# X and the first weights alternately, narrow chunks with their weights loaded and tokens streamed, 32 bytes of padding ahead of the feed-forward operand

## The reference

```python
def dsa_mixer(h, w_in, q_g, k_g, w_out):       # layer a; b is attention without the index
    q, k, v, gate, qi, ki, wi = split_cols(h @ w_in, A_WIDTHS)   # 2048, 512, 512, 2048, 1024, 64, 16 columns
    ...
    score = einsum('bqh,bqhs->bqs', wib, relu(qi . ki))          # index scores, top-64 keys of each query
    _, sel = lax.top_k(score, n_keep)
    ...
    return (jax.nn.silu(gate) * o) @ w_out
```

## Time and profile before

| | us |
|---|---|
| median of 3 runs (2584.04 to 2587.59) | 2585.28 |
| profiled execution, own time | 2575.33 |
| its span in the profile | 2573.9 |
| TensorE busy | 2424.0 (94%) |
| TensorE weight loads | 1978.0 (77%) |
| VectorE busy | 1408.0 (55%) |
| ScalarE busy | 1160.6 (45%) |

### The profile page before, as it was taken

How to read it: one execution, slowest core, us unless ns; L and a number is a source line. 1 busy time by engine, 2 the same in 40 slices (tenths; PEclk the granted TensorE clock), 3 DMA queues, 4 the chain that set the end, 5 groups by cost and what they waited for, 6 DMA issues and landing times.

```text
span 2573.9 us, 27885 instructions
## 1 busy us (share of the span) xinstructions
PE 2424.0 (94%) x11424; PEld 1978.0 (77%) x11424; DVE 1408.0 (55%) x1955; ACT 1160.6 (45%) x1632; POOL 9.6 (0%) x17
## 2 busy tenths in 40 slices
PE   6999999999999987959989889999999999999998
PEld 5777788777788866847877778888888888888886
DVE  4475655655554467576556554565554545454454
ACT  4346644546644543333334444444544344433443
POOL 0000000000000000000000000000000000000000
PEclk9899999999999898989999999999999999999999
DMA  5444355544455442212254336555565555555653
GB/s 186 150 132 130 125 183 184 169 158 131 148 180 166 150 147 82 82 49 82 87 180 145 129 115 194 182 179 189 191 193 183 192 184 194 181 194 183 195 181 114
DMA packets 204223, 400.13 MB, mean 155 GB/s; under 512 B 12736, under 2 KB 12768, under 8 KB 203712
## 3 DMA queue, kind: packets, MB, share of 16 engines
q1 hardware_dynamic: 202016, 391.08, 46.5%
q0 software_dynamic: 1648, 6.32, 0.8%
q10 hardware_dynamic: 432, 0.95, 0.1%
HBM read 396.23 MB, written 2.10 MB: 155 GB/s over the span
## 4 chain that ended last, share of the span: by engine, by line
PE 86%; DVE 9%; ACT 4%; issue 1%; DMA 0%; SPq 0%; ACTq 0%; DVEq 0%
PE ACC L713 25%; PE ACC L715 25%; PE ACC L714 25%; PE TP L394 1%; DVE WL L1492 1%; DVE arena L1249 1%; DVE arena L1278 1%; ACT WH L1001 1%; PE PV L572 1%; PE SC L567 1%; PE PV L575 1%; PE SC L441 1%; PE PV L433 1%; PE SC L624 1%; PE TP L420 1%
## 5 line engine op out<-in xcount | busy, mean ns | idle before, releaser
L1492 DVE TENSOR_TENSOR WL<-W,WH 128x1024 fp32r<-128x1024 f32 (+1 forms) x752 | 901.6, 1202 | 666.0 <-ACT WH L1001 664.2
L1001 ACT ACTIVATE WH<-W 128x1024 fp32r<-128x1024 f32 (+1 forms) x752 | 781.3, 1041 | 822.2 <-PE ACC L715 822.2
L713 PE MATMUL ACC<-WH,XH 128*128 128x512 f32 (+2 forms) x2656 | 1084.6, 408 | 8.2 <-ACT arena L992 4.7
L715 PE MATMUL ACC<-WH,XL 128*128 128x512 f32 (+2 forms) x2656 | 1040.6, 392 | 0.0
L714 PE MATMUL ACC<-WL,XH 128*128 128x512 f32 (+2 forms) x2656 | 1039.6, 391 | 0.0
L713 PEld LDWEIGHTS ACC<-WH,XH 128*128 128x128 f32 x2656 | 509.8, 192 | 120.2 <-issue 13.4
L715 PEld LDWEIGHTS ACC<-WH,XL 128*128 128x128 f32 x2656 | 508.1, 191 | 107.2
L714 PEld LDWEIGHTS ACC<-WL,XH 128*128 128x128 f32 x2656 | 510.3, 192 | 92.8 <-issue 2.0
L713 PE MATMUL ACC<-WH,HH 128*128 128x512 f32 x352 | 139.8, 397 | 0.0
L715 PE MATMUL ACC<-WH,HL 128*128 128x512 f32 x352 | 139.0, 395 | 0.0
L714 PE MATMUL ACC<-WL,HH 128*128 128x512 f32 x352 | 139.0, 395 | 0.0
(11 more groups left out here) (281 smaller groups left out, 1586.4 us busy)
## 6 DMA issues: line engine op xcount, KB each, us to landing
W<-in_w_in SPq DMA_DIRECT2D x84, 1024.0 KB, 5.0
W<-in_a_w_in SPq DMA_DIRECT2D x48, 1024.0 KB, 5.1
W<-in_w_ffn_gate SPq DMA_DIRECT2D x44, 1024.0 KB, 5.2
W<-in_w_ffn_up SPq DMA_DIRECT2D x44, 1024.0 KB, 5.2
W<-in_w_ffn_down SPq DMA_DIRECT2D x44, 1024.0 KB, 5.1
W<-in_b_w_in SPq DMA_DIRECT2D x40, 1024.0 KB, 5.1
W<-in_a_w_out SPq DMA_DIRECT2D x16, 1024.0 KB, 5.0
W<-in_b_w_out SPq DMA_DIRECT2D x16, 1024.0 KB, 5.0
```

The source lines that it names most:

```text
L713: MM(out, hx, WH[:, k, 0:ch.width], start=q == 0 and k == 0, stop=False)
L715: ins = MM(out, lx, WH[:, k, 0:ch.width], start=False, stop=last and k == QK - 1)
L1001: A(M.WH[n % 2][:, ks, 0:ch.width], M.W[n % 4][:, ks, 0:ch.width], ACT.Copy).then_inc(*did("weights_rounded", n, half))
L1492: TT(M.WL[n % 2][:, ks, 0:ch.width], M.W[n % 4][:, ks, 0:ch.width], M.WH[n % 2][:, ks, 0:ch.width].bitcast(F32), ALU.subtract).then_inc(*d ...
```

## The change

Four things. X's column blocks and the first four quads are loaded in turn (X0, W0, X1, W1, ...); the identity is loaded by itself ahead, the rest of the constants later; two of X's blocks are turned ahead of the loop, interleaved with the rounding of quads 0 and 1, and the others, the squares, roots and tables become side work of the first chunk. The two narrow chunks become one quad each of 16 tiles, with the weights (80 or 40 columns) as stationary operand and the 256 tokens streamed; the result, with output columns on the partitions, is copied to M.NT, transposed by the new task `narrow` one visit behind the next chunk's first, and scaled into M.KW or M.NAR. c.nar now follows c.q0, `index` starts four visits behind a.kw and `dn_gates` three behind c.nar. And a tile of 32 bytes per partition is put between the small tiles and the arena.

```diff
-            add("a.kw", one(w, INDEX_COL + IH * ID, ID + IH), "act")
+            add("a.kw", one(w, INDEX_COL + IH * ID, ID + IH), "act", quads=1, tiles=D // P)
...
-    add("c.nar", [(w, GATE_COL, 3 * N2), (w, AB_COL, 2 * DH)], "act", fresh="x.c")
...
+            add(f"c.{n}{i}", one(w, DN_COL + c * DH * HD + i * CH), "act", fresh="x.c" if n + str(i) == "q0" else None)
+            if n + str(i) == "q0":
+                add("c.nar", [(w, GATE_COL, 3 * N2), (w, AB_COL, 2 * DH)], "act", quads=1, tiles=D // P)
...
+    for c in range(2, NC_D):
+        begin(4 * c - 6, "turn", "x.a", c)
+    for c in range(NC_D):
+        begin(8 + c, "squares", "a", c)
+    begin(11, "roots", "a")
+    begin(12, "tables", "a")
     begin(after("a.i0"), "index_rope", 0)
     begin(after("a.i1"), "index_rope", 1)
-    begin(after("a.kw"), "index")
+    begin(after("a.kw") + 1, "narrow", "a.kw")
+    begin(after("a.kw") + 4, "index")
...
-    begin(after("c.nar"), "dn_gates")
+    begin(after("c.nar") + 1, "narrow", "c.nar")
+    begin(after("c.nar") + 3, "dn_gates")
...
+def tiles_of(buffer, ch, half):
+
+    mine = buffer[:, half * HK:(half + 1) * HK, :]
+    if ch.tiles == QK:
+        return mine[:, :, 0:ch.width]
+    n = ch.tiles // 2
+    return mine.rearrange("p k n -> p (k n)")[:, 0:n * ch.width].rearrange("p (k n) -> p k n", k=n)
...
+    sb("to_64_bytes", [P, 8])
...
+    M.NT = {"a.kw": cut(6144, T), "c.nar": cut(12288, T)}
...
-    for c in range(NC_D):
-        sp.dma_start(M.X[:, :, c * CH:(c + 1) * CH], a["x"][0, :, c * CH:(c + 1) * CH].rearrange("(t p) d -> p t d", p=P)).then_inc(*did(f"x_landed{c}", by=16))
     for ch in K.chunks:
         for q in range(ch.quads):
             n = ch.first + q
+            if n < NC_D:
+                cs = slice(n * CH, (n + 1) * CH)
+                sp.dma_start(M.X[:, :, cs], a["x"][0, :, cs].rearrange("(t p) d -> p t d", p=P)).then_inc(*did(f"x_landed{n}", by=16))
...
-                src = a[w][0][row:row + QK * P, col:col + width].rearrange("(k p) n -> p k n", p=P)
+                src = a[w][0][row:row + ch.tiles * P, col:col + width].rearrange("(k p) n -> p k n", p=P)
+                if ch.tiles != QK:
+                    for half in range(2):
+                        ks = slice(half * ch.tiles // 2, (half + 1) * ch.tiles // 2)
+                        sp.dma_start(tiles_of(M.W[n % 4], ch, half)[:, :, place:place + width], src[:, ks, :]).then_inc(*did(f"weights_landed{n % 4}", n, place, half, by=16))
+                    place += width
+                    continue
...
-    pe.wait_ge(*at("consts_landed"))
-    for c in range(NC_D):
+    pe.wait_ge(*at("identity_landed"))
+    for c in range(2):
         for _ in turn("x.a", c):
             pass
...
+    def narrow(name):
+
+        w = K.width_of[name]
+        pe.wait_ge(*at("acc_taken_act", name, 0))
+        wait_empty("TP0")
+        for t in range(TB):
+            ins = TR(TP[0][:, t * w:(t + 1) * w], M.NT[name][0:w, t * P:(t + 1) * P], ident[0:w, 0:w])
+        ins.then_inc(*did("narrow_transposed", name))
+        emptied["TP0"] = ("narrow_taken", name)
+        yield
+
...
+        if ch.tiles != QK:
+            n, out = ch.first, M.ACC[0][0:ch.width, 0:T]
+            pe.wait_ge(*at(*taken[0], 0))
+            for part in range(4):
+                if part % 2 == 0:
+                    pe.wait_ge(*at("weights_rest", n, part // 2))
+                WH, WL = tiles_of(M.WH[n % 2], ch, part // 2), tiles_of(M.WL[n % 2], ch, part // 2)
+                for k in range(part * ch.tiles // 4, (part + 1) * ch.tiles // 4):
+                    j = k % (ch.tiles // 2)
+                    MM(out, WH[:, j, :], hi[:, k, :], start=k == 0, stop=False)
+                    MM(out, WH[:, j, :], lo[:, k, :], start=False, stop=False)
+                    ins = MM(out, WL[:, j, :], hi[:, k, :], start=False, stop=k == ch.tiles - 1)
+                ins.then_inc(*did("multiplied", n, part // 2, part % 2))
+                sides_of(tasks, K.starts, visit, live)
+                visit += 1
+            taken[0] = ("acc_taken_act", ch.name)
+            continue
...
-                    if q == 0 and half == 0 and taken:
-                        pe.wait_ge(*at(*taken, t))
+                    if q == 0 and half == 0 and taken[t]:
+                        pe.wait_ge(*at(*taken[t], t))
...
+        taken = [("acc_taken_" + ch.taker, ch.name)] * TB
...
+    def narrow(name):
+        w, to = K.width_of[name], {"a.kw": M.KW, "c.nar": M.NAR}[name]
+        act.wait_ge(*at("reciprocal_roots", name[0]))
+        act.wait_ge(*at("narrow_transposed", name))
+        for t in range(TB):
+            ins = A(to[:, t, :], TP[0][:, t * w:(t + 1) * w], ACT.Copy, scale=scale_of(name[0], t))
+        ins.then_inc(*did("narrow_taken", name))
+        yield
+
     def take(ch, t):
 
         l, name = ch.name[0], ch.name[2:]
+        if ch.tiles != QK:
+            if t == 1:
+                act.wait_ge(*at("multiplied", ch.first, 1, 1))
+                A(M.NT[ch.name][0:ch.width, :], M.ACC[0][0:ch.width, 0:T], ACT.Copy).then_inc(*did("acc_taken_act", ch.name, 0))
+            return
...
+            act.wait_ge(*at(f"weights_landed{n % 4}", n, ch.width - ch.parts[-1][2], *(() if ch.tiles == QK else (1,))))
...
+        A(tiles_of(M.WH[n % 2], ch, half), tiles_of(M.W[n % 4], ch, half), ACT.Copy).then_inc(*did("weights_rounded", n, half))
...
-    act.dma_start(M.consts[:, :], a["consts"]).then_inc(*did("consts_landed", by=16))
+    act.dma_start(M.ident, a["consts"][:, 0:P]).then_inc(*did("identity_landed", by=16))
...
-    act.dma_start(M.QKG.rearrange("p l n w -> p (l n w)"), a["qk_gains"].partition_broadcast(P)).then_inc(*did("qk_gains_landed", by=16))
     act.wait_ge(*at("gains_landed"))
     for n in range(2):
+        for _ in turn("x.a", n):
+            pass
         for half in range(2):
             round_up(n, half)
-    for c in range(NC_D):
-        for _ in turn("x.a", c):
-            pass
-    for c in range(NC_D):
-        for _ in squares("a", c):
-            pass
-    for _ in roots("a"):
-        pass
+    act.dma_start(M.consts[:, P:], a["consts"][:, P:]).then_inc(*did("consts_landed", by=16))
+    act.dma_start(M.QKG.rearrange("p l n w -> p (l n w)"), a["qk_gains"].partition_broadcast(P)).then_inc(*did("qk_gains_landed", by=16))
...
+        if l == "a":
+            dve.wait_ge(*at("consts_landed"))
+            dve.wait_ge(*at("qk_gains_landed"))
...
-        dve.wait_ge(*at("acc_taken_act", "a.kw", 1))
+        dve.wait_ge(*at("narrow_taken", "a.kw"))
+        dve.wait_ge(*at("index_rotated", 1))
...
     dve.wait_ge(*at("gains_landed"))
-    dve.wait_ge(*at("consts_landed"))
     for n in range(2):
+        for _ in turn("x.a", n):
+            pass
         for half in range(2):
             rest(n, half)
-    for c in range(NC_D):
-        for _ in turn("x.a", c):
-            pass
-    for _ in roots("a"):
-        pass
-    dve.wait_ge(*at("qk_gains_landed"))
-    for _ in tables("a"):
-        pass
```

More of the change, by code:

```diff
@@ L130, in at, with add @@
         return sem, self.told[(name,) + key]
-Chunk = namedtuple("Chunk", "name first quads parts width row0 k0 xs fresh taker")
+Chunk = namedtuple("Chunk", "name first quads parts width row0 k0 xs fresh taker tiles")
 def weight_plan():
     chunks, at = [], 0
-    def add(name, parts, taker, quads=4, row0=0, k0=0, xs="X", fresh=None):
+    def add(name, parts, taker, quads=4, row0=0, k0=0, xs="X", fresh=None, tiles=QK):
         nonlocal at
-        chunks.append(Chunk(name, at, quads, parts, sum(p[2] for p in parts), row0, k0, xs, fresh, taker))
+        chunks.append(Chunk(name, at, quads, parts, sum(p[2] for p in parts), row0, k0, xs, fresh, taker, tiles))
         at += quads
@@ L842, in dn_gates @@
         A(E1, E1, ACT.Ln).then_inc(*did("dn_rates_log"))
-        act.wait_ge(*at("acc_taken_act", "c.nar", 1))
+        act.wait_ge(*at("narrow_taken", "c.nar"))
         A(B, M.NAR[:, :, 3 * N2 + DH:NAR], ACT.Sigmoid)
@@ L996, in round_up @@
         if half == 0:
[L997 removed]
+            act.wait_ge(*at(f"weights_landed{n % 4}", n, ch.width - ch.parts[-1][2], *(() if ch.tiles == QK else (1,))))
         if n >= 2:
             act.wait_ge(*at("multiplied", n - 2, half, 1))
[L1000 to L1003 removed]
+        A(tiles_of(M.WH[n % 2], ch, half), tiles_of(M.W[n % 4], ch, half), ACT.Copy).then_inc(*did("weights_rounded", n, half))
+    tasks = dict(turn=turn, narrow=narrow, squares=squares, roots=roots, keys=keys, queries=queries, attend=attend, index=index, dn_gates=dn_gates, dn_conv=dn_conv,
                  dn=dn, dn_out=dn_out, compress=compress, nsa_keys=nsa_keys, nsa_attend=nsa_attend)
[L1005 removed]
+    act.dma_start(M.ident, a["consts"][:, 0:P]).then_inc(*did("identity_landed", by=16))
     act.dma_start(M.gains[:, :, :], a["norm_gains"]).then_inc(*did("gains_landed", by=16))
[L1007 removed]
     act.wait_ge(*at("gains_landed"))
     for n in range(2):
+        for _ in turn("x.a", n):
```

(9 more changed lines are left out.)

9 lines of the change are left out of this document (2 added, 7 removed).

## The result

| | before | after |
|---|---|---|
| median, us (range, runs) | 2586.39 (2584.04 to 2587.59, 4) | 2547.95 (2544.20 to 2548.62, 4) |
| profiled execution, own time | 2575.33 | 2544.20 |
| its span, mean granted clock | 2573.9, 0.972 | 2542.9, 0.975 |

The ratio of the times is 0.985, 95% interval 0.9832 to 0.9867: 38.4 us faster, where 37.7 were forecast. The profiled spans, though, differ by 31.0 us only. So the sum of stretches and the median have to be looked at apart.

A forecast was written before the change was run, and what follows sets the result against it. TensorE was taken as the bound (86% of the span): its work, idle time and low clock. Gains 14.6 + 9.0 + 1.7 + 5.4 + 7.0 = 37.7 us, from median 2585.3 to 2547.6 us; eight times in ten 2533 to 2562.

The forecast's parts named there:

- The likeliest case: Whole kernel: all four parts work as forecast, 2547.6 us with its own range 2541 to 2555; chance 53%.
- Opening, 14.6: Kernel start: accumulation from 11.4 us, a.i1 begins at 39.4 instead of 54.03; gain 14.6 us, from 9 to 19.
- colder start: Opening's first two quads on TensorE: some 5 us added for the clock's colder start.
- a.kw, 9.0, and 1.7 behind it: a.kw 6.6 instead of 15.6 us; behind it 2.0 back from half clock, less 0.3 for added transposes and copies.
- I cost that at 0: Index work starting four visits later, around the keys and a.q0: no cost, with 4 us either way.
- c.nar, 5.4: c.nar, c.q0 and c.k0 together 60.8 instead of 66.2 us; gain 5.4, from 1 to 10.
- Padding, 7.0: All 1056 HH/HL matmuls 6.7 ns faster each by alignment to 64 bytes; gain 7.0 us, ends 0 and 7.0.
- Arena at 0: Arena matmuls under the new alignment: up to 3 us more gain or a loss of that size, taken as 0.
- which I hold constant: Whole kernel: the profiled execution's 10 us under the median of 2585.3 was assumed to stay the same after.
- The clock did not hold low: Rival: TensorE stays at 1.2 GHz from first matmul to the end of a.k, 2611 us; chance 2%.
- The padding did something: Judges the rival that the 32 bytes of padding do nothing: 2554.6 us; chance 13%.
- The helpers did bind: Rival: ScalarE's order, moved index work and convolution idle time cost 5, 4 and 5 us; 2561 us; chance 15%.

The follow-up runs named there:

- a_same: The changed kernel, unaltered, measured a second time: 2551.35 us, ratio 0.9859 to the kernel before.
- c_pad64: The kernel before with 64 bytes of padding in place of 32, so offsets from a multiple of 64 stay: 2586.36 us, ratio 1.0005.
- w_256: The kernel before with a.kw computed on 256 columns (176 of them unused), same four quads and 96 matmuls: 2578.91 us, ratio 0.9979.
- e_kw: The kernel before plus only a.kw in the new one-quad form, with index four visits behind it: 2571.23 us, ratio 0.9938.
- e_nar: The kernel before plus only c.nar in the new form behind c.q0: 2579.89 us, ratio 0.9976.

## Why the prediction was right, and where not

The likeliest case happened: all four parts work by the mechanisms named. The median is within 0.4 us of the forecast; that closeness is luck, since two errors cancelled. By its steps:

- **Opening, 14.6.** Right; 16.4 measured (a.i1 at 37.60, not 39.4). First accumulating matmul 11.79 for 11.4, releaser ScalarE as said. The 1.8 us are ScalarE's: quad 4's rounding ends at 35.94 for 37.7; the one more rounding is there, quad 5's first half to 36.88, and the take follows at once. The "colder start" cost TensorE less than the 5 us taken: three gaps of 0.42 to 0.59 us instead of 0.23, under 1 us in all.
- **a.kw, 9.0, and 1.7 behind it.** The chunk came at 6.30 for 6.6, the matmul near the 0.12 us taken (5.74 us for 49 records). The formula of the Trainium skill, "TensorE: Matmul & The Clock Gate" (Back-to-back issue gap), would have made 5.2 of it: the row lies on the side of the other rows. Behind it I had 1.7 gained: a.k -5.64, a.v +4.22 and a.q0 +1.02 are 0.4 gained in the one profile, 1.2 in `a_same`. "I cost that at 0" for the index was about 1 us too kind, the top-k in a.q0; the four heads only change places from a.k to a.v.
- **c.nar, 5.4.** c.q0 23.12 for 23.1, c.nar 12.28 for 12.3 and its 5.65 us of idle time for 5.6, ended by the engine that I named. c.k0 failed: 27.98 for 25.4. The idle stretch brought 6.83 us of low clock, 4.92 of them with TensorE at work, so 2.5 lost for my 1.5, and `dn_gates`, which I took over at its cost in c.q0, now waits for VectorE behind the convolution, 2.6 us. Gain 2.8 in this profile, and none in the same kernel's other run with 31.39.
- **Padding, 7.0.** Right in kind: 21.85 for 21.8. All down-projection chunks together gained 5.7. I took the difference of an up- and a down-projection chunk for all 1056 matmuls; the difference of one chunk with itself is 0.55, not 0.63 us (and 0.63 / 96 is 6.6 ns, not 6.7). Arena at 0 was right.
- **Sum and state.** The stretches come to 31 us in the spans, not 37.7. The median fell by 38.4 because "which I hold constant" was wrong: before's profile lay 10 us under the median of 2585.3 (11 under the later 2586.4), after's lies 3.8 under its own. Nothing in the prediction says why the kernel after should run nearer to its profile. The narrow chunks are a part of it at most: c.nar has 13.7 us of low clock in seven of eight profiles, in `c_pad64` the extra time is in other chunks, and `w_256`, which takes the stretch at a.kw away, has 7.0 us less low clock where `e_kw` has 15.0.
- **Rivals.** The clock did not hold low in the opening (1.00 over all 25.81 us, and matmuls 0.23 to 0.24 us apart from 13.23 on). The padding did something. The helpers did bind, 1.2 us at a.i1, 1.0 in a.q0, and most in c.nar and c.k0.

Open: why the medians have 15 to 17 us less low clock where the profiles have 8.5 less, and why the parts' low-clock gains sum to 28.8 us and the whole has 17.2. It is not c.nar's idle time alone: `e_nar` has the same idle time and two low-clock stretches behind it, and still 8.5 less in that column. The low-clock stretches of chunks that no edit touches come and go from run to run, and no run here shows what decides it.

## What to carry to other kernels

Sort each timed run into span x clock and span x (1 - clock) before trusting a sum made from one profile: here the profile stood 10 us off the median, all of it low clock, and the forecast came out right only because the kernel after did not stand as far off. Before giving a longer chunk to a cause, see whether the same chunk is as long in another profile of the same kernel. Look at the clock over matmuls that stream few columns; making them wide, by loading the narrow side as weights or even by adding columns that nobody reads, gave it back here (6.8 us at a.kw, against 4.6 for half the matmuls). When a short chunk is put between two long ones, look at what its take stands behind on the helper's queue, and move that first.

## What the runs showed of the hardware

- A TensorE that is busy 16.82 of 17.01 us with matmuls of 40 columns is granted 0.68 on average, one with 256 columns in the same order 1.00 over 12.08 us. Busy time alone did not keep it at 2.4 GHz here.
- A stationary operand 32 bytes past a multiple of 64 costs 5.7 ns for each matmul of 512 columns (22.41 against 21.86 us for 96), though the weight loads take 18 us in both kernels.
- A kernel's low-clock cost varies by run, with the rest fixed: the rest of before was 2499.6, 2500.0 and 2501.1 us in three sets of runs, while its low-clock part went from 75 to 93 us over these runs, and was 72.1 in its profile. Single chunks show it: a.q1 of one and the same kernel is 33.50 us at 0.95 and 31.95 at 1.00.
- The clock column does not show a slow begin: in the opening of both kernels it has 1.00, but the first 512-column matmuls start some 0.43 us apart (from 12.38 to 13.23, and before from 31.10 to 33.66), as at 0.50 behind c.nar's idle time (866.06, 866.48), and later 0.23 apart.
